# Modulation weights of a two-block transformer in 128x1024 pieces, one DVE pass each, in half as many places

## The chip, the cores and the metric

The kernel runs on one core of a Trainium2 chip. The metric is the device time of one execution in microseconds (us). TensorE (PE) multiplies matrices, PEld is its weight load; VectorE (DVE) and ScalarE (ACT) do the elementwise work; SyncE (SP) issues all transfers from HBM. GpSimd (POOL) is idle.

## The reference, cut to what matters

A block with a pooling and attention mixer is followed by two blocks of another model, on 256 latent tokens of width 1024 and (in the second part) 256 context tokens. Each block is conditioned by modulation vectors. They come from a product of one vector (`silu` of the condition) with a weight of 1024 x 9216:

```
mod = cond @ w_ada[l] + b_ada[l]                     # first part, cond = silu(c)
sh1, sc1, gt1, sh2, sc2, gt2, sh3, sc3, gt3 = split(mod, 9)
u = modulate(rmsnorm(h, g), sh1, sc1)
h = h + 0.5 * gt1 * swiglu(u, w_ffn1_in, w_ffn1_out)
...
m_lat = modulation(c, w_mod[i], b_mod[i])            # second part, i = 0, 1
m_ctx = modulation(c_ctx, w_mod[i], b_mod[i])        # same weights, other condition
x = layer_norm(ALPHA * x + 0.5 * gate * swiglu_2(modulate_2(x, shift, scale)), g, b)
```

There are three such weights (`w_ada`, `w_mod[0]`, `w_mod[1]`), 36 MB each in fp32. The rest, and nearly all of PE's time, is feed-forward layers, a gated MLP, and two attentions in fp32.

## The kernel before

**Matrix products.** Every product is made of three fp32r matmuls (L1184 to L1186, high and low parts). Feed-forward and projection weights come in chunks of 128x1024 (512 KB) in the order of a stream of 606 chunks. A chunk is fetched by SP into one of four `raw` places (L1152), copied to its high part by ACT (L1406), and its low part is subtracted by DVE (L1681, signal `wlo`); only then may PE start on the chunk. The two parts lie in `own`, or in `spare` and `spare_gw` where these are free. Results leave PSUM by ACT and DVE: `up` (L1784), `hlo` (L1789), and the update of the residual `X` (L1662), which also gives the PSUM bank back. PE takes banks in turn, and bank 7 is kept for the modulation.

**Modulation.** DVE forms the modulation vectors, so that PE has nothing to do with them. A section (one of the nine vectors of one weight, 1024 outputs) is a piece of `PIECES`: for each group j of 128 outputs, a 128x1024 slab of the transposed weight is multiplied elementwise by the condition (the same row on all partitions) and summed along its row with the bias as start (L1697). Each slab comes as two halves of 128x512 (256 KB): a section is 16 steps, first the eight first halves, then the eight second halves, which take the first sum from `M` as start. The instruction is two on DVE: the product itself, and the read of the accumulator into a column of `M`. 19 sections are needed for one condition, 11 for two (`whose` has two entries): those read each half twice, the first time with the product itself written to PSUM bank 7, the second time over the weights.

**Places.** The first 32 halves (needed before the first layer) have 16 places in `SCR`; later ones have four: two in `MODS` and two in `SCR` (the latter two in `SQ` between sections 17 and 21, while `SCR` is in use). The load of half m is issued by SP (L1142) when half m-4 has been consumed.

**Order.** A planner in Python writes one list of work items, from which each engine's program is written. `chunk` puts the split of the next chunks, then calls `background`, which adds a `rate` to a credit and spends it on modulation steps: a half of a section for one condition costs 1.0, for two 1.6, and at most two steps are put for one chunk. During a norm (`norming`) none are put. `mod_until` puts all steps that a consumer needs. DVE works strictly in this order. The rates are 1.4 and 0.9 in the first feed-forward layer (`w1`), 1.6 in the projection with rotary embedding (`wpqk`, `wv`), 0.9 in the first attention, 1.5 in its gates (`wg`), and 3.2 in the feed-forward layers `f1` and `f2`. A residual's sums for the next norm are formed while the last output tiles are made: ACT squares them, DVE adds the tiles up (`fold`, L1728 and L1730, into `NT`), and PE sums over partitions (`sums`, L1209 and L1211).

Of the kernel before, what the change touches and what calls it, by code (L numbers as in the profile page):

```python
# [12 lines left out]
ALU = mybir.AluOpType  # L13
# [3 lines left out]
P = 128  # L17
D = 1024
KT = D // P
# [76 lines left out]
def mod_key(which, sec):  # L96

    p = piece_of(which, sec)
    return (16 * p + 15, [w for _, w in PIECES[p][2]].index(which))


def mod_slot(m):
    if m < 32:
        return m % 16
    return 16 + m % 4 + (2 if EARLIER * 16 <= m < MIDDLE * 16 and m % 4 > 1 else 0)
# [34 lines left out]
class Plan:  # L140


    def __init__(self, total):
        self.total = total
        self.stream, self.order = [], []
        self.split = self.fetched = 0
        self.used = {}
        self.place, self.waits, self.deep = {}, {}, False
        self.highs = []
        self.holds = {("ring", i): [] for i in range(RING)}  # L150
        self.uses, self.held, self.turn = [0] * 8, {7}, 0
        self.late = {}
        self.mods = self.mod_loads = 0
        self.mod_limit = EARLIER * 16
# [12 lines left out]
        self.scaled = set()  # L167
        self.last = None
        self.turned = []
# [85 lines left out]
    def mod_fetch(self, done):  # L255
        m = self.mod_loads
        fresh = m < 16 or 32 <= m < 36
        if m >= self.mod_limit or not (fresh or (m - 16 if m < 32 else m - 4) < done):
            return False
        self.put("modload", n=m)  # L260
        self.mod_loads += 1
        return True

    def mod_step(self):
# [7 lines left out]
        while self.mod_fetch(m + 1) and self.mod_loads < m + 18:  # L272
            pass

    def mod_until(self, which, sec):
        while self.mods < 16 * (piece_of(which, sec) + 1):
# [338 lines left out]
def schedule(total):  # L615
# [3 lines left out]
    while p.mod_fetch(0) and p.mod_loads < 16:  # L619
        pass  # L620
# [152 lines left out]
    p.mod_limit = MIDDLE * 16  # L773
# [43 lines left out]
    p.mod_limit = len(PIECES) * 16  # L817
# [111 lines left out]
    assert p.mods == 16 * len(PIECES) and not p.filler  # L929
# [47 lines left out]
def build(nc, T, out, plan, known):  # L977
    ctx = ExitStack()
    with ctx:
# [37 lines left out]
        s_mod = [sem(f"s_mod{i}") for i in range(22)]  # L1017
# [32 lines left out]
        def mod_use(m):  # L1050
# [63 lines left out]
        last_early_mod, last_middle_mod = (EARLIER * 16 - 1, 1), (MIDDLE * 16 - 1, 1)  # L1114
        middle = max(w.id for w in plan.order if w.what == "mod" and w.n == MIDDLE * 16 - 1)
# [3 lines left out]
        def sync(e):  # L1119
            on = Queue(e)  # L1120
            for w in plan.order:
# [9 lines left out]
                elif w.what == "modload":  # L1131
                    m = w.n
                    if 16 <= m < 32:
                        on.wait_ge(s["modded"], (m - 16, len(PIECES[(m - 16) // 16][2]) - 1))
                    elif m >= 36:
                        on.wait_ge(s["modded"], (m - 4, len(PIECES[(m - 4) // 16][2]) - 1))
                    if EARLIER * 16 <= m < MIDDLE * 16:
                        on.wait_ge(s["ulo"], ("l00", KT - 1))
                    elif m >= MIDDLE * 16:
                        on.wait_ge(s["matmul"], last_mix)  # L1140
                    name, sec, _, _ = PIECES[m // 16]
                    e.dma_start(MB[mod_slot(m)], T[name][sec, m % 16]).then_inc(s_mod[mod_slot(m)], 16)  # L1142
# [10 lines left out]
                elif w.what == "maskload":  # L1153
                    on.wait_ge(s["modded"], (31, 0))
# [238 lines left out]
        def scalar(e):  # L1393
# [5 lines left out]
            for w in plan.order:  # L1399
# [109 lines left out]
                elif w.what == "qk1":  # L1509
                    on.wait_ge(s["matmul"], product_key(w))  # L1510
                    on.wait_ge(s["modded"], (31, 0))
# [122 lines left out]
        def vector(e):  # L1634
# [36 lines left out]
            for w in plan.order:  # L1671
# [11 lines left out]
                elif w.what == "mod":  # L1683
                    name, sec, whose, bias = PIECES[w.n // 16]
                    half, j = w.n % 16 // 8, w.n % 8
                    slot = mod_slot(w.n)
                    for a, (who, which) in enumerate(whose):
                        row = who + (0 if w.n < EARLIER * 16 else 2 if w.n < MIDDLE * 16 else 4)
# [462 lines left out]
```

## Time and profile before

| | |
|---|---|
| median of 3 runs | 2561.25 us (2560.92 to 2562.0) |
| the profiled execution, its time | 2559.84 us |
| its span, first to last instruction | 2558.1 us |
| PE busy | 2461.4 us, 96% of the span |
| PEld busy | 2232.2 us, 87% |
| DVE busy | 1848.7 us, 72% |
| ACT busy | 1109.2 us, 43% |
| moved by DMA | 455.77 MB, mean 178 GB/s |

The times of the rows below are in us from the start of the span. The time of the profiled execution is 1.7 us more than its span. A busy share is a mean over stages that have different limits.

### The profile page before, as it was taken

To read this page: it belongs to the slowest core of one execution; us is meant where nothing else is said; L and a number is where in the kernel's file an instruction comes from. 1 tells how busy PE (TensorE), PEld (TensorE's weight loads), DVE (VectorE), ACT (ScalarE), POOL (GpSimd) and SP (SyncE) were. 2 spreads that over 40 slices of the span, in tenths; PEclk is the share of its full clock that TensorE was granted. 3 is DMA by queue.
4 is the path that set the end of the run, shared out by engine and by line. 5 is a ranking of instruction groups with operands and counts; after the bars stand their busy time and mean duration, and the time that the engine had idled before them with its cause. 6 is when DMAs were issued, how large, how long until landed. Compare 5 with 4: busy or idle time off the path is not lost.

```text
span 2558.1 us, 39551 instructions
## 1 busy us (share of the span) xinstructions
PE 2461.4 (96%) x15654; PEld 2232.2 (87%) x15654; DVE 1848.7 (72%) x3589; ACT 1109.2 (43%) x1658; POOL 0.2 (0%) x4
## 2 busy tenths in 40 slices
PE   4999999999999999999999999999999999998998
PEld 3998989999999888788888998888998888877998
DVE  7888987878878746768787669897785444666655
ACT  3444565444463324724232652232652222645444
POOL 0000000000000000000000000000000000000000
PEclk8999999999999999999999999999999999999999
DMA  8887866758867531654444266676373333222653
GB/s 317 309 266 223 256 209 221 259 192 270 293 207 229 182 99 53 216 156 128 149 133 131 82 191 206 193 235 200 96 264 132 112 110 96 67 75 76 199 192 104
DMA packets 161959, 455.77 MB, mean 178 GB/s; under 512 B 17776, under 2 KB 21360, under 8 KB 161776
## 3 DMA queue, kind: packets, MB, share of 16 engines
q1 hardware_dynamic: 161776, 453.26, 54.5%
q8 instruction: 124, 2.03, 0.3%
q14 instruction: 59, 0.48, 0.1%
HBM read 452.14 MB, written 1.05 MB: 177 GB/s over the span
## 4 chain that ended last, share of the span: by engine, by line
PE 77%; DVE 5%; ACT 3%; issue 1%; DMA 1%; ACTq 0%; DVEq 0%; SPq 0%
PE PS L1184 24%; PE PS L1185 24%; PE PS L1186 24%; DVE own L1681 1%; PE PS L1211 1%; PE PS L1338 1%; PE PS L1209 1%; DVE X L1662 0%; ACT own L1406 0%; ACT SCR L1612 0%; DMA SCR<-in_ma 0%; ACT Uh L1467 0%; ACT NT L1471 0%; PE PS L1312 0%; DVE small L1991 0%
## 5 line engine op out<-in xcount | busy, mean ns | idle before, releaser
L1184 PE MATMUL PS<-Uh,own 128*128 128x256 f32 (+1 forms) x2080 | 657.7, 316 | 41.1 <-DVE Ul L1762 20.8
L1185 PE MATMUL PS<-Ul,own 128*128 128x256 f32 (+1 forms) x2080 | 646.5, 311 | 0.0
L1186 PE MATMUL PS<-Uh,own 128*128 128x256 f32 (+1 forms) x2080 | 646.2, 311 | 0.0
L1406 ACT ACTIVATE own<-raw 128x1024 fp32r<-128x1024 f32 x429 | 448.3, 1054 | 374.8 <-PE PS L1186 306.8
L1681 DVE TENSOR_TENSOR own<-raw,own 128x1024 fp32r<-128x1024 f32 x429 | 520.3, 1219 | 67.5 <-ACT own L1406 67.2
L1184 PEld LDWEIGHTS PS<-Uh,own 128*128 128x128 f32 x2080 | 400.7, 193 | 70.1 <-issue 30.7
L1185 PEld LDWEIGHTS PS<-Ul,own 128*128 128x128 f32 x2080 | 401.8, 193 | 19.6 <-issue 0.2
L1186 PEld LDWEIGHTS PS<-Uh,own 128*128 128x128 f32 x2080 | 401.5, 193 | 19.7
L1184 PE MATMUL PS<-Hh,own 128*128 128x256 f32 (+1 forms) x1096 | 349.0, 318 | 1.3 <-DVE Hl L1909 0.7
L1185 PE MATMUL PS<-Hl,own 128*128 128x256 f32 (+1 forms) x1096 | 344.4, 314 | 0.0
L1186 PE MATMUL PS<-Hh,own 128*128 128x256 f32 (+1 forms) x1096 | 344.2, 314 | 0.0
L1662 DVE SCALAR_TENSOR_TENSOR X<-PS,CF,X 128x256 f32<-128x256 f32 x560 | 252.9, 479 | 122.7 <-PE PS L1186 122.1
L1784 DVE TENSOR_TENSOR GT<-SA,PS 128x256 f32<-128x256 f32 (+1 forms) x156 | 76.7, 492 | 338.0 <-PE PS L1186 336.6
L1184 PE MATMUL PS<-Uh,spare 128*128 128x256 f32 (+1 forms) x752 | 245.3, 326 | 4.7 <-DVE Ul L1777 2.9
L1186 PE MATMUL PS<-Uh,spare 128*128 128x256 f32 (+1 forms) x752 | 244.2, 325 | 0.0
L1185 PE MATMUL PS<-Ul,spare 128*128 128x256 f32 (+1 forms) x752 | 244.2, 325 | 0.0
L1184 PEld LDWEIGHTS PS<-Hh,own 128*128 128x128 f32 x1096 | 210.1, 192 | 15.3 <-DVE Hl L1909 0.9
L1185 PEld LDWEIGHTS PS<-Hl,own 128*128 128x128 f32 x1096 | 210.3, 192 | 12.4
L1186 PEld LDWEIGHTS PS<-Hh,own 128*128 128x128 f32 x1096 | 210.1, 192 | 12.2
L1493 ACT ACTIVATE SA<-PS 128x256 f32<-128x256 f32 (+1 forms) x156 | 68.4, 438 | 346.7 <-PE PS L1186 346.3
L1406 ACT ACTIVATE spare<-raw 128x1024 fp32r<-128x1024 f32 x144 | 149.2, 1053 | 123.9 <-PE PS L1186 86.7
L1681 DVE TENSOR_TENSOR spare<-raw,spare 128x1024 fp32r<-128x1024 f32 x144 | 174.4, 1219 | 7.5 <-ACT spare L1406 7.3
(223 smaller groups left out, 3862.4 us busy)
## 6 DMA issues: line engine op xcount, KB each, us to landing
MODS<-in_mm SPq DMA_DIRECT2D x168, 256.0 KB, 3.6
SCR<-in_mm SPq DMA_DIRECT2D x136, 256.0 KB, 3.8
raw<-in_f0i SPq DMA_DIRECT2D x68, 512.0 KB, 4.2
raw<-in_f1i SPq DMA_DIRECT2D x56, 512.0 KB, 3.7
raw<-in_f2i SPq DMA_DIRECT2D x56, 512.0 KB, 3.8
SCR<-in_ma SPq DMA_DIRECT2D x88, 256.0 KB, 5.1
raw<-in_w1i SPq DMA_DIRECT2D x44, 512.0 KB, 4.6
raw<-in_w2i SPq DMA_DIRECT2D x44, 512.0 KB, 4.5
```

The costliest lines, as they stand in the source:

```text
L1184: e.matmul(o, ll, rh, start=start, stop=False)
L1185: e.matmul(o, lh, rl, start=False, stop=False)
L1186: return e.matmul(o, lh, rh, start=False, stop=stop)
L1209: e.matmul(PS[:, w.bank[0], 0:S], ones[:, :], x, start=w.first, stop=w.final, skip_group_check=True)
L1211: e.matmul(PS[:, w.bank[0], S:2 * S], ones[:, :], sq, start=w.first and not w.centred, stop=w.final, skip_group_check=True).then_inc(s["ma ...
L1338: m = e.matmul(PS[:, w.bank[0], tt * P:(tt + 1) * P], VN[:, tt, w.f * P:(w.f + 1) * P], GW[:, g * P:(g + 1) * P], start=True, stop=True)
L1406: e.activation(parts(w.n)[0], raw[:, w.n % RING, :], ACT.Copy).then_inc(s["whi"].tell(w.n), 1)
L1493: e.activation(SA[:, w.j % 2, lo:hi], PS[:, b, lo:hi], ACT.Silu).then_inc(s["gated"].tell(w.j), 1)
L1662: e.scalar_tensor_tensor(out=X[:, k, l:u], in0=PS[:, bank[0], l:u], scalar=cf((st, h))[:, k:k + 1], in1=X[:, k, l:u], op0=ALU.mult, op1=AL ...
L1681: e.tensor_tensor(low, raw[:, w.n % RING, :], high.bitcast(F32), ALU.subtract).then_inc(s["wlo"].tell(w.n), 1)
L1784: e.tensor_tensor(GT[:, w.j % 2, lo:hi], SA[:, w.j % 2, lo:hi], PS[:, b, lo:hi], ALU.mult).then_inc(s["product"].tell(w.j), 1)
```

## The change

A step is now a whole 128x1024 slab (512 KB), 8 steps for a section instead of 16. One condition: one DVE product of 1024 elements. Two conditions: the first still in two products of 512 (their product is written to PSUM bank 7, which has 512 columns), with a wait of DVE on itself between them, then the second condition in one product of 1024 over the weights, with a wait on the two before. The places are eight for the first 16 slabs, then two (`MODS` whole, and 1024 columns of `SCR` or all of `SQ`); the load of slab m is issued when slab m-2 has been consumed. In the planner a step costs 2.0 or 3.2, and the cap of two steps for a chunk is unchanged. The host lays the weights out so that a partition's row of a slab is contiguous (4 KB).

```
 def mod_slot(m):
-    if m < 32:
-        return m % 16
-    return 16 + m % 4 + (2 if EARLIER * 16 <= m < MIDDLE * 16 and m % 4 > 1 else 0)
+    if m < 2 * KT:
+        return m % KT
+    return KT + m % 2 + (1 if EARLIER * KT <= m < MIDDLE * KT and m % 2 else 0)
...
-        fresh = m < 16 or 32 <= m < 36
-        if m >= self.mod_limit or not (fresh or (m - 16 if m < 32 else m - 4) < done):
+        fresh = m < KT or 2 * KT <= m < 2 * KT + 2
+        if m >= self.mod_limit or not (fresh or (m - KT if m < 2 * KT else m - 2) < done):
...
         for _ in range(0 if self.norming else 2):
-            p = self.mods // 16
-            cost = (1.0, 1.6)[len(PIECES[p][2]) - 1] if p < len(PIECES) else 1.0
+            p = self.mods // KT
+            cost = (2.0, 3.2)[len(PIECES[p][2]) - 1] if p < len(PIECES) else 2.0
...
-        MB = [SCR[:, 512 * i:512 * i + 512] for i in range(16)] + [MODS[:, 0:512], MODS[:, 512:1024],
-                                                                   SCR[:, 11264:11776], SCR[:, 11776:12288],
-             SQ[:, 0:2, :].rearrange("p a n -> p (a n)"), SQ[:, 2:4, :].rearrange("p a n -> p (a n)")]
+        MB = [SCR[:, 1024 * i:1024 * i + 1024] for i in range(KT)] + [MODS[:, :], SCR[:, 11264:12288],
+                                                                     SQ[:, :, :].rearrange("p a n -> p (a n)")]
...
-                        if half:
-                            on.wait_ge(s["modded"], (w.n - 8, a))
-                        if not final and w.n and len(PIECES[(w.n - 1) // 16][2]) == 2:
-                            on.wait_ge(s["modded"], (w.n - 1, 0))
-                        e.tensor_tensor_reduce(
-                            out=MB[slot] if final else PS[:, 7, :], in0=MB[slot], in1=COND[row][:, 512 * half:512 * half + 512],
-                            scale=1.0, scalar=o if half else vec(bias, sec * 8 + j), op0=ALU.mult, op1=ALU.add,
-                            accum_out=o).then_inc(s["modded"].tell((w.n, a)), 1)
+                        if final:
+                            if a:
+                                on.wait_ge(s["modded"], (w.n, 0))
+                            e.tensor_tensor_reduce(
+                                out=MB[slot], in0=MB[slot], in1=COND[row], scale=1.0, scalar=vec(bias, sec * 8 + j),
+                                op0=ALU.mult, op1=ALU.add, accum_out=o).then_inc(s["modded"].tell((w.n, a)), 1)
+                            continue
+                        for half in range(2):
+                            part = slice(512 * half, 512 * half + 512)
+                            if half:
+                                on.wait_ge(s["modded"], (w.n, "half"))
+                            elif w.n and len(PIECES[(w.n - 1) // KT][2]) == 2:
+                                on.wait_ge(s["modded"], (w.n - 1, 0))
+                            e.tensor_tensor_reduce(
+                                out=PS[:, 7, :], in0=MB[slot][:, part], in1=COND[row][:, part], scale=1.0,
+                                scalar=o if half else vec(bias, sec * 8 + j), op0=ALU.mult, op1=ALU.add,
+                                accum_out=o).then_inc(s["modded"].tell((w.n, 0 if half else "half")), 1)
...
-        a[n] = w.reshape(2, 512, 9, KT, P).transpose(2, 0, 3, 4, 1).reshape(9, 16, P, 512)
+        a[n] = w.reshape(D, 9, KT, P).transpose(1, 2, 3, 0)
```

Two places in DVE's program show what moves. In these rows an `ISA` with two tiles ahead of the arrow is the product and `ISA M` the read of its accumulator; `SCR`, `MODS`, `SQ` are the places of the weights, `RS`, `NT` and `SCR` hold the condition, and the last name is the start of the sum (`V` the bias, `M` the sum of the first half).

The first place is a section for two conditions in the gated MLP, at its output. Before, with waits:

```order
L1681 TENSOR_TENSOR own<-raw,own 128x1024 [waits s_whi]
L1697 ISA PS,M<-SQ,NT,M 128x512 [waits s_modded,s_mod20]
L1697 ISA M 128x1
L1697 ISA SQ,M<-SQ,RS,M 128x512
L1697 ISA M 128x1
L1789 TENSOR_TENSOR Hl<-GT,Hh 128x512 [waits s_hhi]
```

In the changed kernel, at the same place:

```order
L1680 TENSOR_TENSOR own<-raw,own 128x1024 [waits s_whi]
L1704 ISA PS,M<-SQ,NT,V 128x512 [waits s_mod10]
L1704 ISA M 128x1
L1704 ISA PS,M<-SQ,NT,M 128x512 [waits s_modded]
L1704 ISA M 128x1
L1694 ISA SQ,M<-SQ,RS,V 128x1024 [waits s_modded]
L1694 ISA M 128x1
L1796 TENSOR_TENSOR Hl<-GT,Hh 128x512 [waits s_hhi]
```

One half, in two instructions without a wait of its own, became a slab in three, the second and third of which wait on the instruction ahead of them.

The second place is the end of the feed-forward layer `f1`, where the context half of its last output tiles is updated and added up for the norm. Before, from the step ahead of the first addition:

```order
L1697 ISA SCR,M<-SCR,V 128x512
L1697 ISA M 128x1
L1697 ISA SCR,M<-SCR,V 128x512
L1697 ISA M 128x1
L1662 SCALAR_TENSOR_TENSOR X<-PS,CF,X 128x256
L1728 TENSOR_TENSOR NT<-X 128x256
L1730 TENSOR_TENSOR NT<-SQ 128x256
L1662 SCALAR_TENSOR_TENSOR X<-PS,CF,X 128x256
L1728 TENSOR_TENSOR NT<-NT,X 128x256
L1730 TENSOR_TENSOR NT<-NT,SQ 128x256
L1697 ISA MODS,M<-MODS,SCR,M 128x512
L1697 ISA M 128x1
```

In the changed kernel:

```order
L1694 ISA SCR,M<-SCR,V 128x1024
L1694 ISA M 128x1
L1694 ISA MODS,M<-MODS,SCR,V 128x1024
L1694 ISA M 128x1
L1661 SCALAR_TENSOR_TENSOR X<-PS,CF,X 128x256
L1735 TENSOR_TENSOR NT<-X 128x256
L1737 TENSOR_TENSOR NT<-SQ 128x256
L1661 SCALAR_TENSOR_TENSOR X<-PS,CF,X 128x256
L1735 TENSOR_TENSOR NT<-NT,X 128x256
L1737 TENSOR_TENSOR NT<-NT,SQ 128x256
L1694 ISA SCR,M<-SCR,V 128x1024
L1694 ISA M 128x1
```

Where two halves stood, two whole slabs stand. At these four spots of the layer's end (ahead of the last two tile updates without an addition, and ahead of three pairs of additions) the steps are 2, 2, 2, 2 halves before, and 1, 2, 1, 2 slabs now. The cap of two steps let 1.0 slab through for a chunk before, whatever the credit; at rate 3.2 and cost 2.0 it is now 1.6. What was left of the credit before was spent on 16 halves among the first chunks of the layer `f2`, and none stand there now.

## Rows read from the trace of the kernel before

**Rows 1.** The page's first part: busy time of PE.
```profile
PE 2461.4 (96%) x15654; PEld 2232.2 (87%) x15654; DVE 1848.7 (72%) x3589; ACT 1109.2 (43%) x1658; POOL 0.2 (0%) x4
```

**Rows 2.** Waits of PE over the span: total, times, longest us.
```profile
PE PS L1184 <- DVE Ul L1762: 20.8, 4, 16.1
PE PS L1184 <- DVE own L1681: 12.3, 9, 2.5
```

**Rows 3.** Windows: length, busy us of PE, PEld, DVE, ACT, POOL; PEclk, DMA share, GB/s.
```profile
7.00:16.00 9.00, 0.00 (x0) 0.00 (x0) 9.00 (x27) 0.64 (x2) 0.00 (x0) 1.00 1.05 393
20.50:24.50 4.00, 4.00 (x10) 3.19 (x10) 0.00 (x0) 2.23 (x7) 0.00 (x0) 1.00 1.02 403
...
257.00:312.00 55.00, 51.46 (x407) 50.19 (x405) 51.76 (x114) 25.43 (x43) 0.00 (x0) 1.00 0.79 246
...
1540.00:1740.00 200.00, 200.00 (x884) 165.68 (x883) 185.61 (x420) 55.89 (x66) 0.00 (x0) 1.00 0.68 211
...
1793.00:1806.00 13.00, 11.63 (x96) 11.40 (x95) 12.61 (x36) 3.02 (x8) 0.00 (x0) 1.00 0.59 185
```

**Rows 4.** DVE groups by shape: busy us, mean ns | idle before.
```profile
L1681 DVE TENSOR_TENSOR own<-raw,own 128x1024 fp32r<-128x1024 f32 x429 | 520.3, 1219 | 67.5 <-ACT own L1406 67.2
...
L1789 DVE TENSOR_TENSOR Hl<-GT,Hh 128x512 fp32r<-128x512 f32 x66 | 45.3, 686 | 0.0
```

**Rows 5.** Timeline of the start: start us, us, what [idle before <-releaser].
```profile
19.66 1.33 ACT L1425 ACTIVATE SQ<-X 128x256 f32<-128x256 f32 x4 [12.01 <-DMA X<-in_xT]
...
30.48 0.65 DVE L1697 CUSTOM_DVE_ANT_0 SCR<-SCR,V 128x512 f32<-128x512 f32 x1
...
41.15 0.89 DVE L1756 SCALAR_TENSOR_TENSOR NT<-X,CF,RS 128x256 f32<-128x256 f32 x2
...
42.85 0.55 PE L1184 MATMUL PS<-Uh,own 128*128 128x256 f32 x1 [16.12 <-DVE Ul L1762]
```

**Rows 6.** Timeline of DVE: a wait on its own last instruction.
```profile
308.31 0.42 DVE L1850 TENSOR_TENSOR NT<-PS,SCR 128x256 f32<-128x256 f32 x1
308.64 0.42 DVE L1852 TENSOR_TENSOR SCR<-SCR 128x256 f32<-128x256 f32 x1
309.10 0.42 DVE L1854 TENSOR_TENSOR SCR<-SCR,NT 128x256 f32<-128x256 f32 x1
```

**Rows 7.** Timeline: four of PE's waits, one DVE step.
```profile
312.06 0.39 PE L1184 MATMUL PS<-Uh,own 128*128 128x256 f32 x1 [2.11 <-DVE own L1681]
...
348.00 0.75 DVE L1697 CUSTOM_DVE_ANT_0 MODS<-MODS,SCR,M 128x512 f32<-128x512 f32 x1
...
349.30 0.88 PE L1291 MATMUL PS<-SCR 64*128 64x256 f32 x3 [1.52 <-DVE X L1662]
...
379.20 0.90 PE L1291 MATMUL PS<-SCR 64*128 64x128 f32 x6 [1.43 <-DVE X L1662]
...
725.96 0.70 PE L1211 MATMUL PS<-SQ,ones 128*128 128x256 f32 x2 [0.85 <-ACT SQ L1425]
```

**Rows 8.** Timeline: the first step of `w_mod[1]`, in `f1`.
```profile
1525.61 0.76 DVE L1697 CUSTOM_DVE_ANT_0 PS<-MODS,SCR,V 128x512 f32<-128x512 f32 x1 [4.16 <-DMA MODS<-in_mm]
...
1528.31 0.87 DVE L1662 SCALAR_TENSOR_TENSOR X<-PS,CF,X 128x256 f32<-128x256 f32 x2
...
1531.25 0.47 PE L1184 MATMUL PS<-Uh,own 128*128 128x512 f32 x1 [0.35 <-DVE X L1662]
```

**Rows 9.** The end of `f1`: timeline, and DMA issues with median us to landing.
```profile
1793.48 0.74 DVE L1697 CUSTOM_DVE_ANT_0 MODS<-MODS,SCR,V 128x512 f32<-128x512 f32 x1
...
1795.97 0.74 DVE L1697 CUSTOM_DVE_ANT_0 SCR<-SCR,V 128x512 f32<-128x512 f32 x1
...
1805.53 0.70 PE L1209 MATMUL PS<-NT,ones 128*128 128x256 f32 x2 [1.37 <-DVE NT L1730]
...
MODS<-in_mm SPq DMA_DIRECT2D x4, 256.0 KB, 3.6
SCR<-in_mm SPq DMA_DIRECT2D x4, 256.0 KB, 3.1
```

More of the change, by code:

```diff
@@ L98, in mod_key @@
     p = piece_of(which, sec)
-    return (16 * p + 15, [w for _, w in PIECES[p][2]].index(which))
+    return (KT * p + KT - 1, [w for _, w in PIECES[p][2]].index(which))
 def mod_slot(m):
-    if m < 32:
-        return m % 16
-    return 16 + m % 4 + (2 if EARLIER * 16 <= m < MIDDLE * 16 and m % 4 > 1 else 0)
+    if m < 2 * KT:
+        return m % KT
+    return KT + m % 2 + (1 if EARLIER * KT <= m < MIDDLE * KT and m % 2 else 0)
 U_FROM = {"w1": ("n1", None), "wpqk": ("nm", None), "wv": ("nm", None), "wg": ("nm", None), "w2": ("n2", None),
@@ L153, in __init__ @@
         self.mods = self.mod_loads = 0
-        self.mod_limit = EARLIER * 16
+        self.mod_limit = EARLIER * KT
         self.rate = self.credit = 0.0
@@ L271, in mod_step @@
         self.put("mod", n=m)
-        while self.mod_fetch(m + 1) and self.mod_loads < m + 18:
+        while self.mod_fetch(m + 1) and self.mod_loads < m + KT + 1:
             pass
     def mod_until(self, which, sec):
-        while self.mods < 16 * (piece_of(which, sec) + 1):
+        while self.mods < KT * (piece_of(which, sec) + 1):
             self.mod_step()
@@ L618, in schedule @@
     p.put("condload", q=0, n=0)
-    while p.mod_fetch(0) and p.mod_loads < 16:
+    while p.mod_fetch(0) and p.mod_loads < KT:
         pass
@@ L772, in schedule @@
         p.put("cond", q=who, n=2 + who)
-    p.mod_limit = MIDDLE * 16
+    p.mod_limit = MIDDLE * KT
     p.rate = 2.0
@@ L816, in schedule @@
     p.flush()
-    p.mod_limit = len(PIECES) * 16
+    p.mod_limit = len(PIECES) * KT
     for who in (1, 2):
@@ L928, in schedule @@
         p.put("finish", k=k, n=t["n"], r=LAT)
-    assert p.mods == 16 * len(PIECES) and not p.filler
+    assert p.mods == KT * len(PIECES) and not p.filler
     return p
@@ L1016, in build @@
         s_raw = [sem(f"s_raw{i}") for i in range(RING)]
-        s_mod = [sem(f"s_mod{i}") for i in range(22)]
+        s_mod = [sem(f"s_mod{i}") for i in range(KT + 3)]
         s_cond = [sem(f"s_cond{i}") for i in range(7)]
@@ L1113, in build @@
         last_score1, last_gather1 = (find("score1", k=7).id, 2), (find("gather1", k=7).id, 0)
-        last_early_mod, last_middle_mod = (EARLIER * 16 - 1, 1), (MIDDLE * 16 - 1, 1)
-        middle = max(w.id for w in plan.order if w.what == "mod" and w.n == MIDDLE * 16 - 1)
+        last_early_mod, last_middle_mod = (EARLIER * KT - 1, 1), (MIDDLE * KT - 1, 1)
+        middle = max(w.id for w in plan.order if w.what == "mod" and w.n == MIDDLE * KT - 1)
         def sync(e):
@@ L1132, in sync @@
                     m = w.n
[L1133 to L1137, printed above, removed]
+                    if KT <= m < 2 * KT:
+                        on.wait_ge(s["modded"], (m - KT, len(PIECES[(m - KT) // KT][2]) - 1))
+                    elif m >= 2 * KT + 2:
+                        on.wait_ge(s["modded"], (m - 2, len(PIECES[(m - 2) // KT][2]) - 1))
+                    if EARLIER * KT <= m < MIDDLE * KT:
                         on.wait_ge(s["ulo"], ("l00", KT - 1))
-                    elif m >= MIDDLE * 16:
+                    elif m >= MIDDLE * KT:
                         on.wait_ge(s["matmul"], last_mix)
-                    name, sec, _, _ = PIECES[m // 16]
-                    e.dma_start(MB[mod_slot(m)], T[name][sec, m % 16]).then_inc(s_mod[mod_slot(m)], 16)
+                    name, sec, _, _ = PIECES[m // KT]
+                    e.dma_start(MB[mod_slot(m)], T[name][sec, m % KT]).then_inc(s_mod[mod_slot(m)], 16)
                 elif w.what == "xload":
@@ L1153, in sync @@
                 elif w.what == "maskload":
-                    on.wait_ge(s["modded"], (31, 0))
+                    on.wait_ge(s["modded"], (2 * KT - 1, 0))
                     e.dma_start(CM, T["c1"]).then_inc(s_mask, 16)
@@ L1510, in scalar @@
                     on.wait_ge(s["matmul"], product_key(w))
-                    on.wait_ge(s["modded"], (31, 0))
+                    on.wait_ge(s["modded"], (2 * KT - 1, 0))
                     dst = q_sb[:, w.k, :] if w.k < 6 else k_sb[:, w.k - 6, :]
@@ L1683, in vector @@
                 elif w.what == "mod":
-                    name, sec, whose, bias = PIECES[w.n // 16]
-                    half, j = w.n % 16 // 8, w.n % 8
-                    slot = mod_slot(w.n)
+                    name, sec, whose, bias = PIECES[w.n // KT]
+                    j, slot = w.n % KT, mod_slot(w.n)
                     for a, (who, which) in enumerate(whose):
-                        row = who + (0 if w.n < EARLIER * 16 else 2 if w.n < MIDDLE * 16 else 4)
+                        row = who + (0 if w.n < EARLIER * KT else 2 if w.n < MIDDLE * KT else 4)
                         final = a == len(whose) - 1
```

## The prediction

> **What bounds the kernel now.** I read the page first: PE is busy for 2461.4 us of 2558.1, DVE for 1848.7 [rows 1]. The change touches only DVE and the transfers, so it can move the end only where PE waits for DVE, or where DVE has no room left. Next I read PE's waits: the largest that end at DVE's work are one of 16.1 us at the start and nine for the low part of a chunk, 12.3 us in all [rows 2]. Then the windows: where PE waits, DVE is full or nearly so (51.8 of 55 us in 257 to 312, 12.6 of 13 us in 1793 to 1806), and in 1540 to 1740 DVE is at 185.6 of 200 us while PE never waits [rows 3]. Last I read the timeline around each wait, to see what stands in DVE's queue ahead of what PE waits for. The total of DVE's busy time tells little here; its order and its room at these places decide.
>
> **The price of a step.** At the start, 16 halves run one behind the other from 30.48 to 41.15 us, with the reads of the accumulator beneath the next product: 0.667 us each [rows 5]. 512 more elements cost 1219 - 686 = 533 ns in another DVE operation [rows 4]; the product of 1024 is not in the trace, and its bounds are 0.67 + 0.53 = 1.20 us and twice a half, 1.33 us. I take 1.20, since the 0.13 us that don't grow with the length should be paid once. A slab for one condition then saves 0.13 us, not the 0.75 us that a product shows as its own length.
>
> For two conditions there are three products instead of four, but two of them now wait for the instruction ahead. Of three operations of one size, the second starts 0.33 us behind the first, on which it doesn't wait, and the third 0.46 us behind the second, on which it does [rows 6]: 0.13 us for a wait. Behind a read of the accumulator it may be a little more; I take 0.15 each (bounds 0 and 0.3). Four halves took 2.67 us; now 2 x 0.67 + 1.20 + 2 x 0.15 = 2.84, or 0.17 us more. Over the program: 152 slabs for one condition x -0.13 = -20 us, 88 for two x 0.17 = +15 us. DVE's work hardly changes.
>
> The Trainium skill (VectorE: DVE Perf Modes, The DRAIN you can't avoid) says that a semaphore behind each DVE operation costs nothing extra. The two starts above differ, 0.46 against 0.33 us, so this trace speaks against that. By the rule a slab for two conditions would save 0.13 us, DVE would lose 32 us of work, and the sum below would be lower by 0.3 us.
>
> **Start (gain).** The queue of transfers is full: 393 GB/s with 2 KB rows, 403 with the 4 KB rows of `raw` [rows 3]. X is behind 4.19 MB of modulation weights, so it should land 10.67 - 10.41 = 0.3 us earlier; ACT's squares start with it at 19.66 [rows 5], and the chain behind them moves along. Then 16 halves of 10.67 us become 8 slabs of 9.6, right ahead of the first norm, for which PE waits until 42.85 [rows 5]: -1.1. Together **-1.3 us**. Bounds: 0 (slab at 1.33 us, X not earlier) and -1.8.
>
> **257 to 312 (gain).** DVE is full and PE waits 2.11 us at 312.06 for a low part [rows 3, 7]. Between these times 24 halves stand in DVE's order and 12 slabs now: 16.0 - 14.4 = **-1.6 us**, less than the wait, so PE gets it whole. From the issue of a slab's load (when the slab two before is done) to its turn it is two chunks less a slab, and a chunk takes 3.2 us here (407 matmuls by 24 a chunk, in 55 us [rows 3]): 5.2 us, enough for a landing of 4.0 to 4.5 (below). Bounds 0 and -1.6.
>
> **Odd places (loss).** At rate 0.9 a half stood behind each chunk; now a slab stands behind every other. Where a half of 0.67 us stood right ahead of what PE waits for, at 348.00 ahead of the wait of 1.52 us at 349.30, and likewise ahead of those at 379.20 and 725.96 [rows 7], a slab stands now: 3 x 0.53 = **+1.6 us**. The places that lose their step are ones at which PE didn't wait. Bounds: 0 (ACT is late there too) and +2.5.
>
> **First step of the last weight, at 1525 (loss).** DVE stands 4.16 us for a load issued just before, then four halves, then the two updates of X that give a PSUM bank back at 1528.31; PE is short of banks there and waits 0.35 us at 1531.25 [rows 8]. A slab's last byte comes later by 256 KB at about 400 GB/s, 0.65 us, and the slab takes 0.17 more: **+0.8 us**. The same happens at 1071, where no update of X stands behind it: 0.
>
> **End of `f1` (loss).** This is the largest term. From 1793.48 to the last fold DVE has no idle time to speak of, and PE waits for that fold 1.37 us until 1805.53 [rows 3, 9]. Up to it, 8 halves (5.3 us) become 6 slabs (7.2 us), since the cap of two steps no longer holds the rate back: +1.9. And two of the slabs come second in a pair, whose load is issued only when the slab two before is consumed. A load of 256 KB lands after 3.1 to 3.6 us there [rows 9]; I add 0.65 and take 4.0 us. The first slab ends at 1793.48 + 1.20 = 1794.7, so the load for the third lands at 1798.7; the second starts at 1795.97 [rows 9], so DVE would want the third at 1797.2: 1.5 us. With that, the fifth slab's end and two pairs of updates between, the same sum gives 0.7 us at the last pair. In all 1.9 + 1.5 + 0.7 = 4.1, and I take **+4.0 us**. Bounds: +1.9 with every load in time, +5 with 4.5 us for a landing. PE's tiles there are done before, so nothing covers it. The loads that go away from the start of `f2` (16 halves) give nothing back: PE doesn't wait there.
>
> **Priced at nothing.** In 1540 to 1740 one slab for two conditions goes with each chunk, 37 in all: +6 us of DVE work into 14.4 us of room [rows 3]. Without that cover it would be lost whole. The rest of `w1`, `w2`, `f0`, the gated MLP and `f2` have more room, and the low parts there are ready two or more chunks ahead. SP's queue keeps its order; a fetch of `raw` stands behind a load that waits on DVE just as before, and in the gates stage, where DVE waits now and then for a half, the longer landing and the cheaper slabs about cancel.
>
> **Sum.** -1.3 - 1.6 + 1.6 + 0.8 + 4.0 = +3.5 us. Against the profiled execution's 2559.84 us that is 2563.3; that execution is 1.4 us below the median of 2561.25, so a median of about **2564.8 us**, +0.14%. Less than 0.2% (5 us) is about what a measurement of this kernel can't tell from no change.
>
> **Rivals.**
> *DVE becomes the bound in the middle of `f1`* (slower). It decides once 37 slabs take more than the 14.4 us of room: 0.39 us more a slab, so from 0.26 us for each wait on itself. At 0.4 us each the slab is 0.67 us dearer, 24.8 - 14.4 = +10.4 us on top: 2575. Against it stand the 0.13 us of [rows 6]. Chance 0.10.
> *Slabs come late wherever three chunks in a row have one* (slower). The load for the third is issued when the first ends, and behind two low parts of 1.22 [rows 4] and a slab of 1.20, some 3.6 us later, it is wanted; at 4.0 to 4.5 us that is 0.4 to 0.9 us. This happens some eight times in the start of `w1`, behind 312 us and in the gates. If PE sees them all: +6, 2571. For it: DVE is full there; against it: low parts are mostly ahead. The Trainium skill (DMA: Bandwidth & Descriptors, Rules for kernel authors) says to issue a load early and wait on it late, and half the places make the issue later; in the rows the price is the 4.16 us of [rows 8]. Chance 0.15.
> *The end of `f1` is hidden* (the other side). If the loads land in time and PE has a tile left to do, the largest term goes: -0.5, 2560.8; without the odd places as well, -2.1, 2559.2. Against it: PE waits there already. Chance 0.18.
> The forecast itself has 0.52, with 2561 to 2568 as its own range; 0.05 is left for what I don't see.
>
> **Chances and range.** Faster by over 0.2% (below 2556.1) needs the third rival and a gain that I haven't found: 0.08. Slower by over 0.2% (above 2566.4): the first two rivals and the upper part of the forecast: 0.35. The rest, 0.57, is within 0.2%. The range 2558.5 to 2571 takes in the third rival and the second, and leaves out the first.
>
> **What the profile after would show.** Right: the wait before the first matmul group down from 16.1 to about 15 us; the start of that group near 41.5; the wait at 312 down by 1.6; the wait for the fold at the end of `f1` up from 1.37 to about 5, with DVE waiting on `in_mm` just before; the 1024 product 1.2 us from start to start. Wrong: a product of 1024 at 1.33 us; PE waits inside 1540 to 1740; no DMA wait of DVE at the end of `f1`; or new waits of PE for low parts in `w1` and the gates, which would make the time longer than I say.

## The result, and the profile after

| | median us | runs | ratio to before, 95% interval |
|---|---|---|---|
| before, beside the first comparison | 2561.09 (2560.33 to 2562.86) | 6 | |
| changed kernel | 2570.34 (2566.84 to 2572.54) | 6 | 1.0034 (1.0024 to 1.0044) |
| changed kernel, second comparison (before: 2559.91, 28 runs) | 2567.49 (2566.10 to 2570.70) | 6 | 1.0027 (1.0016 to 1.0039) |

The changed kernel is slower by some 8 us, 0.3%. The profiled execution took 2568.87 us with a span of 2567.1, 9.0 more than before. The page of the changed kernel, first part, queue and chain:

```profile
PE 2462.2 (96%) x15654; PEld 2232.3 (87%) x15654; DVE 1840.3 (72%) x3109; ACT 1108.0 (43%) x1658; POOL 0.2 (0%) x4
...
q1 hardware_dynamic: 127216, 453.24, 53.6%
...
PE PS L1183 24%; PE PS L1184 24%; PE PS L1185 24%; DVE own L1680 1%; PE PS L1210 1%; PE PS L1337 1%; PE PS L1208 1%; DMA MODS<-in_mm 1%; DVE X L1661 1%; ACT own L1405 1%; ACT SCR L1611 0%; DMA SCR<-in_ma 0%; ACT Uh L1466 0%; ACT NT L1470 0%; DMA SCR<-in_mm 0%
```

DVE does 8.4 us less than before [rows 1] and the kernel is slower: as before, DVE's total says little. The chain names the loads of `in_mm` now, which it didn't before; the sums (L1208, before L1209) have 1% in both. The waits of PE name the place (total, times, longest, in us):

```profile
PE PS L1183 <- DVE Ul L1769: 19.8, 2, 15.7
...
PE PS L1183 <- DVE own L1680: 11.6, 11, 2.5
PE PS L1208 <- DVE NT L1737: 7.1, 1, 7.1
```

Against [rows 2], the first group's wait fell from 16.1 to 15.7, the waits for low parts from 12.3 to 11.6, and one wait for the folds at the end of `f1` rose from 1.37 [rows 9] to 7.1. Windows of the changed kernel (length, busy us of PE, PEld, DVE, ACT, POOL; then PEclk, DMA share, GB/s):

```profile
7.00:16.00 9.00, 0.00 (x0) 0.00 (x0) 8.26 (x13) 0.37 (x2) 0.00 (x0) 1.00 1.02 405
...
1540.00:1740.00 200.00, 200.00 (x884) 165.62 (x883) 191.30 (x345) 55.99 (x66) 0.00 (x0) 1.00 0.66 211
1804.00:1811.00 7.00, 0.00 (x0) 0.00 (x0) 6.88 (x16) 1.25 (x3) 0.00 (x0) 0.67 0.50 168
1811.00:1816.70 5.70, 5.69 (x20) 5.13 (x21) 0.83 (x2) 0.93 (x3) 0.00 (x0) 0.51 0.32 110
```

The last two are the end of `f1`. First PE does nothing for 7 us while DVE is full; then, in the 5.7 us behind the wait, PE is busy but finishes 20 matmuls at a granted clock of 0.51, mostly its lower level of 1.2 GHz. Before, the same stretch behind its wait had 37 at full clock (windows of the kernel before):

```profile
316.50:384.40 67.90, 64.88 (x479) 60.08 (x478) 58.74 (x119) 45.12 (x70) 0.00 (x0) 0.95 0.66 216
1805.50:1811.20 5.70, 5.67 (x37) 5.36 (x38) 1.75 (x5) 1.46 (x5) 0.00 (x0) 1.00 0.20 69
```

So the loss there has two parts: 7.09 - 1.37 = 5.7 us of waiting, and 2.6 us of work at the low clock. The timeline of DVE ahead of it, in the changed kernel, and the loads of 1780 to 1812 with their median us to landing:

```profile
1796.79 1.27 DVE L1694 CUSTOM_DVE_ANT_0 SCR<-SCR,V 128x1024 f32<-128x1024 f32 x1
...
1800.52 1.28 DVE L1694 CUSTOM_DVE_ANT_0 MODS<-MODS,SCR,V 128x1024 f32<-128x1024 f32 x1 [2.45 <-DMA MODS<-in_mm]
...
1803.86 1.28 DVE L1694 CUSTOM_DVE_ANT_0 SCR<-SCR,V 128x1024 f32<-128x1024 f32 x1
...
1807.19 1.27 DVE L1694 CUSTOM_DVE_ANT_0 MODS<-MODS,SCR,V 128x1024 f32<-128x1024 f32 x1
1808.39 0.08 DVE L1694 DVE_READ_ACCUMULATOR2_ANT M<- 128x1 f32 x1
...
1808.59 1.28 DVE L1694 CUSTOM_DVE_ANT_0 SCR<-SCR,V 128x1024 f32<-128x1024 f32 x1
...
1811.01 1.22 PE L1208 MATMUL PS<-NT,ones 128*128 128x256 f32 x2 [7.09 <-DVE NT L1737]
...
SCR<-in_mm SPq DMA_DIRECT2D x6, 512.0 KB, 4.4
MODS<-in_mm SPq DMA_DIRECT2D x5, 512.0 KB, 4.4
```

**Where the 9 us came from.** Take the instant at which PE first uses a given chunk of weights in both profiles; the difference is how late the changed kernel is there. It is -1.1 us at chunk 0 (42.82 to 41.72), -3.0 at chunk 86 (316.48 to 313.46), -2.1 at chunk 149 (539.98 to 537.92), -1.2 at chunk 252 (853.29 to 852.04), -0.2 at chunk 386 (1531.22 to 1530.98), **+8.1** at chunk 438 (1824.64 to 1832.72), +9.3 at chunk 517 (2207.28 to 2216.57), and nothing is added behind that. So the changed kernel leads for 1530 us and loses 8.3 us at the end of `f1`; the 1.2 us ahead of chunk 517 are the clock (below). I call this difference the lag below.

### The profile page after: what moved, and what is told of

The parts are those of the page before. It is cut to its first block, busy times and chain, and to the rows that moved or that the text cites. A ratio compares the mean times of both kernels' runs of the same rounds, so it can differ in the third digit from the quotient of the medians.

```text
span 2567.1 us, 38508 instructions
## 1 busy us (share of the span) xinstructions
PE 2462.2 (96%) x15654; PEld 2232.3 (87%) x15654; DVE 1840.3 (72%) x3109; ACT 1108.0 (43%) x1658; POOL 0.2 (0%) x4
## 4 chain that ended last, share of the span: by engine, by line
PE 75%; DVE 6%; ACT 3%; DMA 2%; issue 1%; ACTq 0%; DVEq 0%; SPq 0%
PE PS L1183 24%; PE PS L1184 24%; PE PS L1185 24%; DVE own L1680 1%; PE PS L1210 1%; PE PS L1337 1%; PE PS L1208 1%; DMA MODS<-in_mm 1%; DVE X L1661 1%; ACT own L1405 1%; ACT SCR L1611 0%; DMA SCR<-in_ma 0%; ACT Uh L1466 0%; ACT NT L1470 0%; DMA SCR<-in_mm 0%
```

## The experiments

Two theories for the end of `f1`. **A, pacing:** the cap of two steps a chunk now lets 1.6 slabs through where 1.0 came before, so slabs come in pairs and six slabs, not eight halves, stand ahead of the folds. **B, places:** a load of 512 KB with only two places is late at any pace. **C** is about the second part: the low clock follows from the long wait. Each kernel was timed beside the kernel before on the same chip.

**Cap of one slab a chunk** (e1_cap)

```
-        for _ in range(0 if self.norming else 2):
+        for _ in range(0 if self.norming else 1):
```

> The changed kernel with one number changed: at most one slab of modulation weights per chunk of weights (it was two), so that the single slabs come one a chunk as the kernel before had two halves a chunk, and four slabs stand in the last tiles of f1 instead of six. Nothing is left out of the computation. Theory A (pacing: the loss at the end of f1 is made by the two extra slabs there and the lateness that pairs of slabs bring along): the gap of TensorE at the start of the sums falls from 7.1 us to 1 to 2.5 us, the stretch of half clock behind it (2.6 us) goes with it, and the time is 2561 to 2563 us, 7 to 9 below the changed kernel. Theory B (loads of 512 KB in two places are late at any pacing): the gap stays above 4 us and the time above 2566 us.

Measured: 2564.70 us (11 runs), ratio 1.0013 (1.0004 to 1.0021).

```profile
PE PS L1208 <- DVE NT L1737: 1.1, 1, 1.1
```

The wait is back to before's, the clock behind it is 1.00 (window of 1812 to 1818), and the lag doesn't grow there. DVE's waits for `in_mm` between 1740 and 1811 show the mechanism. In the changed kernel:

```profile
DVE MODS L1694 <- DMA MODS<-in_mm: 7.5, 4, 2.5
DVE SCR L1694 <- DMA SCR<-in_mm: 3.9, 4, 2.4
```

With the cap there is none at all, in the same two places and with the same loads of 512 KB. Theory B falls: two places are enough for one slab a chunk, and too few for pairs. The median came out above the 2561 to 2563 that I expected; what else adds is taken up below.

**The kernel before with four halves a chunk** (e2_before_four)

```
-        for _ in range(0 if self.norming else 2):
+        for _ in range(0 if self.norming else 4):
```

> The kernel before, pieces of 128x512 and all four places, with the cap raised from two to four pieces a chunk: the same number of columns' sums stands at the end of f1 as in the changed kernel (twelve halves instead of eight), with no slab, no self-wait and four places. Theory A (pacing): a gap of 4 to 7 us at the start of the sums at the end of f1, and 2565 to 2569 us. Theory B (it is the slab's length and the two places): the gap stays under 3 us and the time is within 1.5 us of the kernel before. A result between them divides the loss: what the twelve halves cost alone is pacing, the rest is the slab.

Measured: 2568.10 us (5 runs), ratio 1.0032 (1.0019 to 1.0045).

```profile
1810.00:1815.70 5.70, 5.70 (x21) 5.11 (x22) 0.75 (x2) 0.93 (x3) 0.00 (x0) 0.54 0.20 67
```

PE's wait for the folds is 5.31 us, 3.9 more than before with the same places and pieces, and the window behind it has the low clock too (0.54). Between 1740 and 1811 DVE now waits for its loads, though they are of 256 KB in four places; in the kernel before it doesn't wait for one there:

```profile
DVE MODS L1697 <- DMA MODS<-in_mm: 3.7, 4, 1.6
DVE SCR L1697 <- DMA SCR<-in_mm: 1.7, 2, 1.3
```

Nothing of the slabs is in this kernel, and it is as slow as the changed one. This is the strongest evidence for A.

**Half of the bytes, all of the work** (e4_halfload)

```
-  e.dma_start(MB[mod_slot(m)], T[name][sec, m % KT])
+  part = 512 if 209 <= m < 230 else 1024
+  e.dma_start(MB[mod_slot(m)][:, 0:part], T[name][sec, m % KT, :, 0:part])
```

> The changed kernel with slabs 209 to 229 (those of f1 for which one condition is summed, the last six of them in its last tiles) loaded by half: 128x512 of each come, and the other half of the columns that are summed is what stood in the place, so these sums leave out half of the weights. VectorE's instructions and all waits stay. Theory D (the loads: a slab of 512 KB lands 3.6 to 4.4 us after its issue, and two places do not cover it): the waits of 2.45, 2.4 and 2.1 us for slabs between 1740 and 1801 us halve or vanish, the gap at the end of f1 falls from 7.1 to 2 to 4 us, and 3 to 6 us are won. Rival (the work: six slabs of 1.2 us and their order alone): the gap falls by under 1 us.

This kernel leaves out half of those weights, so it doesn't compute the function; it is for timing alone. Measured: 2567.03 us (9 runs), ratio 1.0028 (1.0018 to 1.0038), 0.5 to 3.3 us below the changed kernel, so the 3 to 6 us of theory D are not shown in the time. Its waits of DVE for loads in the same stretch and PE's wait for the folds:

```profile
DVE SCR L1695 <- DMA SCR<-in_mm: 2.1, 1, 2.1
DVE MODS L1695 <- DMA MODS<-in_mm: 1.7, 2, 0.9
...
PE PS L1209 <- DVE NT L1738: 3.5, 1, 3.5
```

DVE's waits went from 11.4 us to 3.8, and PE's from 7.09 to 3.50. So of the 5.7 us by which the wait grew, 3.6 are late loads and 2.1 are the work of six slabs: no wait for a load is left here behind 1797 us. The clock behind fell nonetheless (0.52 from 1810.8 to 1816.5), so the low clock's part remained.

**A busy TensorE in the wait** (e3_busy)

```
+  if w.first and w.j < 0 and w.n == 9:
+      for _ in range(24):
+          e.matmul(PS[:, w.bank[0], 0:P], ones[:, :], ones[:, :], start=True, stop=True)
   if w.j < 0:
       x, sq = NT[:, lo // S, 0, :], NT[:, lo // S, 1, :]
```

> The changed kernel with 24 matmuls of ones by ones (128x128, about 0.21 us each, 5.1 us in all), written to the bank that the sums at the end of f1 clear with their first matmul, put on TensorE just ahead of the wait of those sums for VectorE's fold. Nothing of the computation changes. They lie inside the 7.1 us gap. Theory C (the 2.6 us behind the gap are the lower clock that 7 us without a matmul brings): the granted clock is 1.0 from 1811 to 1817 us, the remaining gap is about 2 us, and the span is 2.4 to 2.8 us shorter than the changed kernel's (some 2566 to 2568 us in the median). Rival: the clock falls whatever fills the gap, or the slow stretch has another cause: no change of the span over 0.5 us beyond the spread of the changed kernel's runs.

Timeline of PE there, and the window behind:

```profile
1807.55 5.52 PE L1203 MATMUL PS<-ones 128*128 128x128 f32 x48
1814.46 0.70 PE L1211 MATMUL PS<-NT,ones 128*128 128x256 f32 x2 [1.39 <-DVE NT L1740]
...
1815.00:1821.00 6.00, 6.00 (x44) 5.74 (x43) 2.26 (x6) 1.59 (x6) 0.00 (x0) 1.00 0.22 82
```

The clock stays at 1.00, and the lag grows by 5.4 us at this place instead of 8.3. C holds in the profile: the low clock behind the wait cost 2.6 to 2.9 us there. In the time it doesn't show: 2568.08 us (5 runs, 2566.41 to 2570.69) lies between the changed kernel's 2567.49 and 2570.34. A gain of 2.6 us is of the size of what the clock does elsewhere from one run to the next, which the next run shows.

**The changed kernel once more** (e0_after_again)

> The changed kernel once more, on the same chip as the three below, since the lower clock falls at other places from run to run and moves single executions by 4 us. Both theories: 2567 to 2571 us, a gap of 7.1 us at the start of the sums at the end of f1.

Measured: 2567.49 us. The wait at the folds is 6.75 us. Two windows of this profile, each behind a norm:

```profile
1447.30:1453.30 6.00, 5.25 (x19) 4.26 (x20) 2.13 (x5) 4.73 (x8) 0.00 (x0) 0.72 0.28 85
2210.80:2216.80 6.00, 5.24 (x33) 4.62 (x34) 3.14 (x6) 2.93 (x9) 0.00 (x0) 1.00 0.29 86
```

The same instructions in the first profile of the same kernel:

```profile
1447.90:1453.90 6.00, 5.27 (x33) 4.66 (x34) 2.46 (x6) 5.31 (x10) 0.00 (x0) 1.00 0.25 86
2211.40:2217.40 6.00, 5.55 (x23) 4.59 (x24) 1.99 (x3) 2.52 (x6) 0.00 (x0) 0.72 0.27 85
```

One program, the same wait of 1.53 us at the start of each window, and the low clock stands at one place in one execution and at the other in the next. Each is worth 1.2 to 1.6 us of lag. Several such places would make single runs of one kernel lie 4 to 8 us apart, as they do; that this is the whole cause is not shown, since only one run of each kernel has a profile. So the comparisons below take the profile's waits beside the medians.

**Cap, and no slab in the last tiles of `f1`** (e5_cap_hold), and **the same hold alone in the kernel before** (e5_before_hold)

```
 # outer_halves
+        held, self.norming = self.norming, self.norming or st == "f1"
         self.drain(half(CTX))
+        self.norming = held
```

> The changed kernel with the cap of one slab a chunk, and in addition no slab at all during the context half of f1's last output tiles: the four slabs that the cap leaves there follow in f2. Nothing is left out of the computation. Theory A (all that is lost at the end of f1 is VectorE's work for slabs ahead of the folds): the gap of 1.1 us at the sums, which is left with the cap alone, goes to under 0.3 us, nothing new shows in f2 over 0.5 us, and the time is 1 to 1.5 us below the cap alone (2564.7 there; 2562.5 to 2564). Rival: the twelve slabs one a chunk in f2 make VectorE late there, a new wait for the low part of the weights of 1 us or more takes the gain back.

> The kernel before with nothing changed but that no piece stands during the context half of f1's last output tiles. Theory A: its gap of 1.37 us at the sums goes, 1 to 1.5 us below the kernel before. Rival: the sixteen halves that follow two a chunk in f2 make waits there, no gain.

Measured: 2563.30 us, ratio 1.0010 (1.0002 to 1.0019), and 2561.13 us, ratio 1.0005 (0.9996 to 1.0014), 11 runs each; of the second, one took 2726.47 us, and the median of the other ten is 2560.77. In both, the wait at the folds is gone and the lag falls there by 1.6 us, as expected; it grows again by 1.8 and 0.7 us up to chunk 462, where the moved pieces stand and a low part is ready only 0.05 us ahead of its use (3.8 us in the kernel before). So the rival holds for this edit: little or nothing is left of it. Against the kernel before on its own chip the cap with the hold is 3.4 us above, the cap alone 3.3.

**Slabs for the first 15 sections only** (e6_hybrid15), **with the hold** (e7_hybrid_hold), **slabs for the first 8 sections with the hold** (e8_hybrid8_hold, e10_hybrid8_again)

```
+SLABBED = 15          # or 8
+def base_of(p):
+    return KT * p + KT * max(0, p - SLABBED)
...
             cost = (1.0, 1.6)[len(PIECES[p][2]) - 1] if p < len(PIECES) else 1.0
+            if p < SLABBED:
+                cost *= 2
...
+                    if p >= SLABBED:
+                        half = (m - base_of(p)) // KT
+                        src = src[:, 512 * half:512 * half + 512]
```

> Slabs of 128x1024 for the first 15 sections (one condition each, up to 853 us) and from there the kernel before's pieces of 128x512 in two passes, four places and its pacing: from chunk 218 on its order is that of the kernel before. The full computation. By the differences of TensorE's position in the profiles, the slabs win 1.1 us at the start, 1.2 to 2.3 us between 257 and 312 us, and lose 0.5 to 1 us in attention and in the folds at 722 us; the dual slabs lose 0.5 at 852 us, 1 us at 1531 us, and the pacing 8.3 us at 1811 us. Theory A (the early slabs are worth something, all loss is behind 850 us): 0.5 to 2.5 us below the kernel before. Rival (what the early slabs win is the placing of clock drops, chance from run to run, and gaps elsewhere give it back): within 0.5 us of the kernel before, or above it.

> The mixed version above, and in addition no piece during the context half of f1's last output tiles (the eight halves that stand there follow in f2). Theory A: the gap of 1.4 us at the sums goes, 1 to 1.4 us below the mixed version, 2 to 3.5 us below the kernel before. Rival: the pieces moved into f2 make a wait there that takes it back; no gain over the mixed version.

> Slabs for the first 8 sections alone (up to 315 us, ahead of the context half of the attention), the kernel before's pieces behind them, and no piece during the context half of f1's last output tiles. The full computation. Theory A: it keeps the 0.8 to 1.1 us of the start and the 1.7 to 2.3 us of 257 to 312 us, does without the 2.5 us that slabs cost in attention in each profile so far (TensorE's waits at 355 and 358 us for L1661 and L1900), and has the 1.4 us of the held pieces: 2.5 to 4.5 us below the kernel before. Rival (a gain ahead of the attention is slack that the attention takes back): the lag after the attention is 0 again, and the time is 0 to 1.5 us below before, as with 15 sections.

> The 8-section mix with its hold once more, since its first comparison (2559.09 against 2560.44 us, interval 0.9985 to 1.0003) leaves it open whether it beats the kernel before. Theory A (its profile has 2.9 us less idle time of TensorE than the kernel before, and the lower clock falls by chance): 1 to 3 us below before again. Rival: no difference, 0 to 1 us on either side.

| slabs | median us | before | ratio, 95% interval |
|---|---|---|---|
| 15 sections | 2561.81 | 2559.91 | 1.0005 (0.9996 to 1.0014) |
| 15 sections, hold | 2560.82 | 2559.91 | 1.0000 (0.9992 to 1.0009) |
| 8 sections, hold | 2559.09 | 2560.44 | 0.9994 (0.9985 to 1.0003) |
| 8 sections, hold, again | 2558.19 | 2561.06 | 0.9988 (0.9979 to 0.9997) |

With 15 sections the wait at the folds is before's 1.37, and the whole loss behind 850 us is gone, but no gain is left: 0.5 to 2.5 us were expected, 2 to 3.5 with the hold, and both intervals take in no change. Part of what the slabs win ahead of the attention they lose in it. To see this, take profiles whose granted clock is 1.00 from chunk 86 to chunk 102. The kernel before with the hold (halves):

```profile
318.90:384.30 65.40, 61.93 (x478) 57.39 (x478) 57.46 (x117) 44.55 (x70) 0.00 (x0) 1.00 0.66 220
```

The changed kernel (slabs), in its first and its second profile:

```profile
313.50:381.00 67.50, 61.98 (x479) 57.40 (x478) 55.64 (x99) 45.29 (x70) 0.00 (x0) 1.00 0.66 216
314.40:381.70 67.30, 62.03 (x479) 57.44 (x478) 55.66 (x99) 45.33 (x70) 0.00 (x0) 1.00 0.65 217
```

The 8-section version in its second profile, which has halves here too:

```profile
314.10:381.60 67.50, 61.93 (x478) 57.38 (x477) 57.60 (x117) 45.26 (x70) 0.00 (x0) 1.00 0.63 216
```

The same matmuls and the same 62 us of PE in all. With slabs it takes 1.9 to 2.1 us more than the first line, though DVE is busy 1.8 us less. But not all of this is the slabs. From chunk 95 to chunk 102 both profiles with slabs take 33.2 us and both with halves 32.2: 1.1 us for slabs. The rest stands at the first wait for X, ahead of chunk 95, and there halves do no better. That wait is 1.56 us in the changed kernel; with halves it is 1.52 us in the kernel before, 2.64 in the 8-section version, and 0.54 only in the profile of the first line, which came to this stretch 2.5 us later than the kernel before. (The kernel before in its own profile took 67.9 us for the stretch, at a clock of 0.95.)

The 8-section version stops with the slabs ahead of the attention, and loses at its first wait what it saves behind it: that it does better in the attention, which was the reason to try it, is not shown. It is the fastest of all in both comparisons, by 1.4 and 2.9 us, where 2.5 to 4.5 were expected; only the second interval leaves out no change, so a gain of about 0.1% is likely, not certain, and where it comes from is open.

**No piece in the attention** (e9_hybrid8_hold2)

```
     n1 = 8
+    p.norming = True
     for i in range(n1 + 3):
 ...
+    p.norming = False
     p.rate = 1.5
```

> As the 8-section mix with its hold, and in addition no piece in the attention of the latents (chunks 91 to 112); the 28 or so halves follow two a chunk from chunk 113 on. Theory A (in the attention VectorE's own chain sets the pace, and every piece there is on it): TensorE's waits of 1.5 us each for X at 349 and 379 us shrink by the 0.67 us of a piece each, 1 to 2.5 us won by chunk 112. Rival: between chunks 113 and 137 the low part of the weights is already waited for (slack 0.05 us at chunk 133), so the moved pieces cost there as much or more, up to 0.67 us each for ten pieces: the time is up to 5 us above the 8-section mix. The rival is the likelier for the sum, theory A for the attention itself.

Measured: 2563.72 us (10 runs), ratio 1.0014 (1.0005 to 1.0024). Waits of PE in it from 340 to 500 us:

```profile
PE PS L1217 <- DVE own L1714: 5.4, 3, 2.5
PE PS L1217 <- DVE Hl L1962: 1.9, 2, 1.4
PE PS L1324 <- DVE X L1695: 1.7, 2, 1.0
PE PS L1334 <- DVE X L1695: 0.8, 1, 0.8
```

and in the 8-section version without this edit:

```profile
PE PS L1322 <- DVE X L1693: 3.9, 2, 2.5
PE PS L1215 <- DVE Hl L1960: 1.1, 1, 1.1
PE PS L1215 <- DVE own L1712: 0.9, 2, 0.6
```

Both halves of the expectation came true: the attention's waits for X fell from 3.9 to 2.5 us, and those for low parts behind it rose from 0.9 to 5.4. The lag went from -1.8 us at chunk 85 to -5.5 at chunk 102, and to +3.1 by chunk 149. From chunk 86 to 102 it took 64.5 us at a granted clock of 1.00, 3.0 less than the 8-section version at that clock (67.5 above). In the time it is 4.6 us above that version on the same chip.

## Why the prediction was right, and what was off

The sign of the sum, the place of the largest term and the range held; the predicted median of 2564.8 was too low by 5.5 us in the first comparison and 2.7 in the second. The likeliest class, within 0.2%, is not what came: the change costs 0.3%, on the side that had 0.35. The forecast's own range, 2561 to 2568, has the second median and not the first. That the wider range, which reached to 2571 for the sake of the second rival, holds 2570.34 as well is in part luck, for that rival didn't come. By its steps:

- **Price of a step.** Right. At the start the slabs follow one another at 31.61, 32.82, 34.02: 1.20 us. Eight took 30.50 to 40.06 = 9.56 us (predicted 9.6). A slab for two conditions began at 1734.32 in the changed kernel, its second half at 1735.17, its second pass at 1736.02, and the last read of the accumulator at 1737.23: 2.91 us against 2.84 predicted. A wait on itself is 0.85 - 0.67 = 0.18 us, not 0.15. The Trainium skill (VectorE: DVE Perf Modes, The DRAIN you can't avoid) says that a semaphore behind a DVE operation costs nothing extra; these rows, 0.85 against 0.67 us, speak against it too.
- **Start.** Predicted -1.3, measured -1.1. X was not earlier (ACT's squares at 19.68, before 19.66 [rows 5]), though the queue moved 405 GB/s instead of 393 [rows 3]; the gain is DVE's alone.
- **257 to 312.** Predicted -1.6; the waits at 306.8 and 312 fell by 0.77 and 0.67, 1.4 together. The lag won 1.9 us from chunk 0 to 86. Some of this is the clock, which fell in before's profile behind the wait at 312 and didn't in the changed one's.
- **Odd places.** Predicted +1.6, of it 2 x 0.53 in the attention. The size there was about right: 1.1 us from chunk 95 to 102, and up to 1.0 more at the first wait, which the runs leave open (above). The places were wrong. The waits named (349.30, 379.20) hardly grew, 1.52 to 1.56 and 1.43 to 1.51. PE waits 1.26 us at 358.38 (rows below), 0.7 in the kernel before with the hold, and 0.40 at 374.93, where that one doesn't wait. The wait of 0.79 at 355.42 is no price of a slab: with halves it is 0.8 there. The third, at 725.96, stayed at 0.85; a new one of 0.65 us for a fold stands 2 us ahead of it, and the lag grows by 0.3 from chunk 149 to 218 where 0.53 was predicted.
- **First step of the last weight.** Predicted +0.8. The wait named, at 1531.25, stayed at 0.35; a new one for X, of 1.02 us, stands 2 us ahead of it (0.90 in the second profile), and the lag grows by 1.0 from chunk 350 to 386. The size was right, the place not.
- **Middle of `f1`, priced at nothing.** Right: PE 200.00 of 200 us, DVE +5.7 us (predicted +6). The first rival falls.
- **End of `f1`.** The term that was mis-sized: +4.0 predicted, **+8.3** measured. The mechanism was the predicted one. The work was 1.9 predicted, 2.1 measured. The late loads were 2.2 predicted (1.5 and 0.7), 3.6 measured: the first wait was 2.45, for its load landed 4.4 us after its issue at 1796.11, not 4.0, and DVE wanted it 2.1 us behind the end of the first slab, not 2.5; the second wait didn't come; and, which was not in the sum, DVE was 1.1 us late already at the slab ahead, for slabs came in pairs from 1740 on and it waited 2.14, 2.38 and 2.42 us for a third one; I had worked out only the last tiles. The low clock behind, 2.6 us, was not in the sum at all.
- **Second rival** (slabs late wherever three chunks in a row have one, +6 us by the gates). It didn't come. Between 40 and 850 us DVE's waits for `in_ma` grew from 4.5 to 7.3 us, but PE's waits for low parts fell there from 10.3 to 9.2, and the lag at chunk 218 is -1.8. At the end of `f1` late loads need a pair: with the cap of one no wait for `in_mm` is left between 1740 and 1811. The Trainium skill (DMA: Bandwidth & Descriptors, Rules for kernel authors) says to issue a load early and wait on it late; this case agrees: two slabs in a row leave little between the issue of a load and its use, and DVE waits 11.4 us in that stretch, with one a chunk 0.
- **Third rival** (end of `f1` hidden): false.

What stays open: the cap of one slab is still 3.3 us above the kernel before. In its profile the lag grows by 1.1 us from chunk 86 to 102 (granted clock 0.95 in both), by 2.5 from chunk 350 to 386 (a wait of 0.83 at 1532.93, and the low clock behind 1440: 0.94 over 30 us, where before has 1.00), by 1.6 from chunk 445 to 462 and by 1.5 up to chunk 517, at a clock of 0.98. The third is a cost of the cap itself: it moves eight slabs into the start of `f2`, where PE now waits 0.86 and 0.20 us for low parts. I have not separated these by a run. What sets the length of the first wait in the attention is open too.

The timeline of the changed kernel for the odd places; the second wait has a slab on DVE just ahead of what it ends with:

```profile
355.42 0.85 PE L1300 MATMUL PS<-ident,GW 128*128 128x128 f32 x6 [0.79 <-DVE X L1661]
355.62 1.28 DVE L1694 CUSTOM_DVE_ANT_0 SCR<-SCR,V 128x1024 f32<-128x1024 f32 x1
...
357.96 0.28 DVE L1900 TENSOR_TENSOR Hl<-PS,Hh 64x128 fp32r<-64x128 f32 x1
...
358.38 0.36 PE L1183 MATMUL PS<-Uh,own 128*128 128x256 f32 x1 [1.26 <-DVE Hl L1900]
```

## What to carry to other kernels

When the unit of background work is doubled, look at every count that was written in units: here a limit of two steps a chunk had been the brake that kept the load in front of a norm small, and the doubling released it. A larger unit is cheap where the engine runs it back to back, and dear where a short step stood just ahead of something that another engine waits for; a total of busy time shows neither. And a wait of TensorE of several microseconds is to be priced with what its clock does behind it.

## What the runs showed of the hardware

- Behind waits of 7.09, 5.31 and 3.50 us at the folds the granted clock was 0.51 to 0.54 over the next 5.7 us, behind one of 6.75 us 0.73, and the lag grew there by 6.8 us instead of 8.3 (so the clock took 1.4 us instead of 2.6); behind 1.37, 1.1 and 1.39 us there it stayed at 1.00. With matmuls of no use in the wait, it stayed at 1.00.
- Behind short waits it is not settled by the program: with the same 1.53 us ahead the stretch was at 1.00 or 0.72, in two executions of one kernel. The Trainium skill (TensorE: Matmul & The Clock Gate, Part 1: The HAM clock gate) says that how much of one kernel runs at the low clock at its start differs from run to run; these rows show the same behind waits inside a kernel. The kernel before alone ranged from 2557.59 to 2565.42 us in 19 runs beside the first experiments.
- A load of 512 KB landed after 4.4 us (median, at the end of `f1`), one of 256 KB there after 3.1 to 3.6 [rows 9]. The product of 1024 elements with its sum runs at 1.20 us from start to start, the one of 512 at 0.67, and at 0.85 where it waits for the one ahead.
